# Handing out unnormalised x in the first block of a two-block fp32 transformer, with the inverse root multiplied in behind the products and half of the residual additions on GpSimd

## What is computed

```python
def rmsnorm(x, g):
    return x * rsqrt(mean(x * x, axis=-1) + EPS) * g

h = rmsnorm(x, norm_mix_pre[l])
a_in, b_x, b_b, b_c, q, k, v, gate_in = split(h @ w_in[l])
merged = ...                       # pooling, convolution and dilated attention, gated
x = x + rmsnorm(merged @ w_out[l], norm_mix_post[l])
h = rmsnorm(x, norm_mem_pre[l])
mem_n = rmsnorm(mem, norm_memkv[l])
x = x + rmsnorm(memory_cross_attention(h, mem_n, w_mq[l], w_mkv[l], w_mo[l]), norm_mem_post[l])
h = rmsnorm(x, norm_ffn_pre[l])
ua, ub = split(h @ w_up[l])
y = (silu(causal_dwconv(ua, conv_ffn_w[l])) * ub) @ w_down[l]
x = x + rmsnorm(y, norm_ffn_post[l])
```

## Time and profile before

| what | value |
|---|---|
| median of three runs | 3808.35 us (3804.64 to 3812.05) |
| the profiled execution | 3807.09 us, its span 3805.3 us |
| TensorE, products busy | 3605.1 us, 95% of the span |
| VectorE busy | 2018.6 us, 53% |
| ScalarE busy | 1504.8 us, 40% |
| GpSimd busy | 241.7 us, 6% |
| mean granted TensorE clock | 0.986 |

### The profile page before, as it was taken

The page is one execution under the profiler, slowest core; times in us unless marked ns, Lnnn a source line. Parts: engine busy times, 40 slices in busy tenths (PEclk is TensorE's granted clock), DMA queues, the critical chain, the costliest instruction groups (busy, mean ns, idle before and its releaser), DMA issues.

```text
span 3805.3 us, 52598 instructions
## 1 busy us (share of the span) xinstructions
PE 3605.1 (95%) x19348; PEld 2957.6 (78%) x19348; DVE 2018.6 (53%) x3396; ACT 1504.8 (40%) x2302; POOL 241.7 (6%) x384
## 2 busy tenths in 40 slices
PE   8999989999999998899999988899999998899998
PEld 6788876887787887688778776788888777667886
DVE  4634466777764455577774465442333444644344
ACT  4344354332324534533235366432122334743233
POOL 0000000001000000000000052000000002610000
PEclk9999999999999999999999999999999999999999
DMA  3222322446332233144551102111211122112322
GB/s 132 93 72 95 98 80 83 147 140 195 119 99 78 71 106 108 42 149 139 191 164 56 50 2 42 45 50 61 66 61 61 55 63 58 31 45 78 99 94 83
DMA packets 113071, 333.14 MB, mean 88 GB/s; under 512 B 32792, under 2 KB 33688, under 8 KB 112408
## 3 DMA queue, kind: packets, MB, share of 16 engines
q1 hardware_dynamic: 74112, 265.23, 21.6%
q0 software_dynamic: 14400, 52.44, 4.3%
q10 hardware_dynamic: 24408, 13.46, 1.6%
HBM read 328.99 MB, written 6.00 MB: 88 GB/s over the span
## 4 chain that ended last, share of the span: by engine, by line
PE 82%; DVE 8%; ACT 6%; issue 2%; DVEq 1%; POOL 0%; ACTq 0%; DMA 0%; POOLq 0%; SPq 0%
PE PS L602 14%; PE PS L604 13%; PE PS L603 13%; PE PS L984 10%; PE PS L985 10%; PE PS L987 10%; PE PS L1112 1%; PE PS L677 1%; PE PS L771 1%; ACT PB L1675 1%; ACT FULL_P L1675 1%; ACT L1366 1%; PE PS L783 1%; DVE HVAL L1958 1%; DVE Y L2371 1%
## 5 line engine op out<-in xcount | busy, mean ns | idle before, releaser
L1914 DVE TENSOR_TENSOR WL<-RAW,WH 128x1024 fp32r<-128x1024 f32 x494 | 604.5, 1224 | 573.5 <-ACT WH L1330 568.2
L1330 ACT ACTIVATE WH<-RAW 128x1024 fp32r<-128x1024 f32 x494 | 521.2, 1055 | 636.3 <-PE PS L987 350.2
L602 PE MATMUL PS<-HHI,WH 128*128 128x512 f32 x1632 | 651.2, 399 | 24.5 <-DVE HLO L1951 16.2
L604 PE MATMUL PS<-HHI,WL 128*128 128x512 f32 x1632 | 639.9, 392 | 0.0
L603 PE MATMUL PS<-HLO,WH 128*128 128x512 f32 x1632 | 638.0, 391 | 0.0
L984 PE MATMUL PS<-H2HI,WH 128*128 128x512 f32 (+1 forms) x1336 | 470.0, 352 | 0.0
L985 PE MATMUL PS<-H2LO,WH 128*128 128x512 f32 (+1 forms) x1336 | 446.6, 351 | 0.0
L602 PEld LDWEIGHTS PS<-HHI,WH 128*128 128x128 f32 x1632 | 307.4, 188 | 105.3 <-issue 19.7
L987 PE MATMUL PS<-H2HI,WL 128*128 128x512 f32 (+1 forms) x1336 | 387.4, 350 | 0.0
L604 PEld LDWEIGHTS PS<-HHI,WL 128*128 128x128 f32 x1632 | 307.1, 188 | 70.5
L603 PEld LDWEIGHTS PS<-HLO,WH 128*128 128x128 f32 x1632 | 307.3, 188 | 64.3 <-issue 0.5
(11 more groups left out here) (353 smaller groups left out, 5737.0 us busy)
## 6 DMA issues: line engine op xcount, KB each, us to landing
RAW<-in_stream SPq DMA_DIRECT2D x494, 512.0 KB, 3.6
MODW<-in_modw POOLq DMA_DIRECT2D x96, 512.0 KB, 4.6
bias_rows<-in_rpb ACTq DMA_DIRECT2D x8, 476.2 KB, 6.7
X<-in_x SPq DMA_DIRECT2D x4, 512.0 KB, 5.5
MEM<-in_mem ACTq DMA_DIRECT2D x2, 1024.0 KB, 4.9
CROW<-in_crow POOLq DMA_DIRECT2D x4, 512.0 KB, 4.7
BIAS<-bias_rows ACTq DMA_DIRECT2D x8, 224.0 KB, 5.0
GRID<-bias_rows ACTq DMA_DIRECT2D x8, 224.0 KB, 4.6
```

The lines of the kernel that those rows point to most:

```text
L602: nc.tensor.matmul(out, WH[:, slot, b * P:(b + 1) * P], hi, start=start, stop=False)
L604: return nc.tensor.matmul(out, WL[:, slot, b * P:(b + 1) * P], hi, start=False, stop=stop)
L1330: A(WH[:, d, :], RAW[:, s, :], ACT.Copy).then_inc(high_split, 1)
L1914: TT(WL[:, d, :], RAW[:, s, :], WH[:, d, :].bitcast(F32), ALU.subtract).then_inc(split_ready, 1)
```

## The change

It has these parts.

1. At M0, M1, F0 and F1 `raw_pair` takes the place of `sum_squares` and `chunk_pair`: for each chunk TensorE sums the squares (SQ_RAW, three buffers), then multiplies the unnormalised high and low parts with the first unit, and two chunks behind with the second. ScalarE makes x times gain in high precision, VectorE the rest (`raw_low`), as soon as each chunk of X is there.
2. At M0 and M1 only these two units are raw. They go to bank 1 and 4, and the normalised parts follow in HHI and HLO while they are read (`raw_read`). The next two units are a `chunk_pair` on them. The two U chunks are multiplied by the inverse root in the pooling. The weight splits for the next two units move into `norm_apply`; `memory_sums` stays behind the pair.
3. At Q0 and Q1 all four query units are raw. The pair comes ahead of the statistics product. VectorE multiplies each with the inverse root on its way out of PSUM.
4. At F0 and F1 all 44 units are raw. GpSimd multiplies UA and the result of Silu by the inverse root (RF): two operations of 128x512 for each pair of units. Its loads of modulation rows go between these. The second modulation reduction moves ahead of the last subtraction, and a weight split ahead of the convolution.
5. In the five residuals ahead of a raw norm, GpSimd adds every second chunk.
6. At the start, SyncE loads the parameters first and two weight units between the halves of x.

```diff
+SQ_RAW = place("SQ_RAW", [P, 3, T], at=S0)
+RF = place("RF", [P, T], at=S0 + 3 * T + 16)
@@ sync
+            sp.dma_start(PAR[:], params1).then_inc(par_in, 16)
             for j in range(4):
                 sp.dma_start(X[:, 2 * j:2 * j + 2, :], x[:, 2 * j:2 * j + 2, :]).then_inc(x_part[j], 16)
+                if j == 1:
+                    first_units(0, SPLIT_AHEAD)
+            first_units(SPLIT_AHEAD, RAW_SLOTS)
@@ gpsimd
+            def odd_additions(n):
+                for j in range(KB // 2):
+                    b = 2 * j + 1
+                    pool.wait_ge(y_scaled, n * (KB // 2) + j + 1)
+                    nc.gpsimd.tensor_tensor(X[:, b, :], X[:, b, :], Y[:, b, :], ALU.add).then_inc(x_odd, 1)
+                odd_additions(3 * l)
+                odd_additions(3 * l + 1)
+                load_modulation(0)
+                load_modulation(1)
+                for j in range(FF):
+                    pool.wait_ge(taken[0], UP_TAKEN[l] + j + 1)
+                    nc.gpsimd.tensor_tensor(UA[:, 0, 8:8 + T], UA[:, 0, 8:8 + T], RF[:], ALU.mult).then_inc(up_scaled, 1)
+                    if j:
+                        load_modulation(j + 1)
+                    pool.wait_ge(silu_ready, l * FF + j + 1)
+                    nc.gpsimd.tensor_tensor(FC[:, 0, :], FC[:, 0, :], RF[:], ALU.mult).then_inc(gate_scaled, 1)
+                for u in range(FF + 1, MOD_LAYER):
+                    load_modulation(u)
+                if l < DEPTH - 1:
+                    odd_additions(3 * l + 2)
@@ tensor
+            def raw_pair(hi, lo, sums, more, release=False, clock=18):
+                slots = [(m.n["units"] + x) % SLOTS for x in range(2)]
+                keep_clock(clock)
+                for slot in slots:
+                    set_in(slot)
+                for k in range(KB + RAW_LAG):
+                    if k < KB:
+                        if sums:
+                            m.add("sq")
+                            pe.wait_ge(sq_ready, m.at("sq"))
+                            nc.tensor.matmul(FLAT[:, 6 * T:7 * T], ONES[:], SQ_RAW[:, k % 3, :], start=k == 0, stop=k == KB - 1,
+                                             skip_group_check=True).then_inc(sq_summed, 1)
+                        if k == 0:
+                            pe.wait_ge(split_ready, m.at("units", 2))
+                        m.add("lo")
+                        pe.wait_ge(lo_ready, m.at("lo"))
+                        last = products(bank(3 * slots[0] + more), slots[0], k, hi[:, k, :], lo[:, k, :], k == 0, k == KB - 1)
+                        if k == KB - 1:
+                            unit_out(last)
+                    if k >= RAW_LAG:
+                        c = k - RAW_LAG
+                        last = products(bank(3 * slots[1] + more), slots[1], c, hi[:, c, :], lo[:, c, :], c == 0, c == KB - 1)
+                        if release and c < KB - 1:
+                            last.then_inc(raw_read, 1)
+                unit_out(last)
-                chunk_pair(HHI, HLO)
+                raw_pair(HHI, HLO, True, 1, release=True, clock=18 if l else 0)
+                chunk_pair(HHI, HLO, behind=1)
                 if l == 0:
                     memory_sums()
+                raw_pair(HHI, HLO, False, 1)
                 statistics(T)
-                chunk_pair(HHI, HLO)
                 for _ in range(HEADS - 2):
-                    chunk(HHI, HLO)
+                    chunk(HHI, HLO, behind=1)
-                sum_squares(T)
-                chunk_pair(HHI, HLO)
+                raw_pair(HHI, HLO, True, 0)
@@ scalar
+            def raw_and_squares(gain, arrived):
+                for k in range(KB):
+                    arrived(k)
+                    if k >= 3:
+                        act.wait_ge(sq_summed, m.at("sum", k - 2))
+                    A(SQ_RAW[:, k % 3, :], X[:, k, :], ACT.Square, scale=D ** -0.5).then_inc(sq_ready, 1)
+                    A(HHI[:, k, :], X[:, k, :], ACT.Identity, scale=gain(k)).then_inc(hi_ready, 1)
+            def x_landed(k):
+                if k == 4:
+                    for _ in range(SPLIT_AHEAD):
+                        split_high()
@@ scalar, at M0 and M1
+                root(T, summed=True)
+                unit_spent()
+                norm_high((0, 1))
+                unit_spent()
+                norm_high(range(2, KB))
+                for c in range(2):
+                    A(U[:, c, :], bank(3 * p + 1), ACT.Copy).then_inc(taken[p], 1)
                 if l == 0:
                     memory_squares()
@@ vector
+            def raw_low(k, gain):
+                m.add("hi")
+                dve.wait_ge(hi_ready, m.at("hi"))
+                STT(HLO[:, k, :], X[:, k, :], gain(k), HHI[:, k, :].bitcast(F32), ALU.mult, ALU.subtract).then_inc(lo_ready, 1)
             def norm_apply(gain):
                 for k in range(KB + 1):
+                    if k < KB - 1:
+                        m.add("rawr")
+                        dve.wait_ge(raw_read, m.at("rawr"))
+                    if k in (1, 3):
+                        split_low()
             def residual(gain, add, between=None, raw=None):
                 for k in range(0, KB, 2):
+                    scaled_y = [STT(Y[:, b, :], Y[:, b, :], par(gain + b), RS[:, 0:T], ALU.mult, ALU.mult) for b in (k, k + 1)]
+                        scaled_y[1].then_inc(y_scaled, 1)
+                        TT(X[:, k, :], X[:, k, :], Y[:, k, :], ALU.add).then_inc(x_ready, 2)
+                    if k and raw is not None:
+                        for b in (k - 2, k - 1):
+                            raw_low(b, raw)
+            for k in range(KB):
+                if k == 4:
+                    for _ in range(SPLIT_AHEAD):
+                        split_low()
+                raw_low(k, mix_gain(0))
@@ vector, in rope_tables
-                split_low()
                 dve.wait_ge(sin_ready, 2)
@@ vector, at the queries
+                def head_in(c):
+                    TT(QM[:, c, :], bank(3 * p + (c < 2)), RS[:, 0:T], ALU.mult).then_inc(taken[p], 1)
@@ vector, the up loop
+                        split_low()
+                        dve.wait_ge(up_scaled, m.at("ups"))
                         (the convolution as before)
+                        modulation(at(j), 0, b)
                         split_low()
+                        dve.wait_ge(gate_scaled, m.at("gts"))
                         TT(FT[:, 0, :], FC[:, 0, :], bank(3), ALU.mult).then_inc(taken[1], 1)
+                        modulation(at(j), 1, b)
+                        low(FLO[:, at(j), :], FT[:, 0:1, :], FHI[:, at(j), :])
```

More of the change, by code:

```diff
@@ L613, in unit_out, with set_in @@
                 m.add("units")
-            def set_in(p):
-                pe.wait_ge(taken[p], m.at(f"use{p}", 1))
+            def set_in(p, behind=0):
+                pe.wait_ge(taken[p], m.at(f"use{p}", 1 - behind))
                 m.add(f"use{p}")
@@ L1604, in _ @@
                         act.wait_ge(taken[1], m.at("use1", 1))
-                        A(FHI[:, bass.ds(2 * i + b, 1), :], FT[:, 0:1, :], ACT.Copy).then_inc(hi_ready, 1)
+                        A(FHI[:, b:b + 1, :] if first else FHI[:, bass.ds(2 * i + (b + 2), 1), :], FT[:, 0:1, :], ACT.Copy).then_inc(hi_ready, 1)
+                up_chunks(0, first=True)
+                with m.loop(act, FF // 2 - 1, units=4, use0=2, use1=2, conv=2, **QUAD) as i:
+                    up_chunks(i)
                 def of_down(k, dst, n):
@@ L2205, in _, with post @@
                     dve.drain()
[L2207 removed]
+                def post(gain, raw):
                     root_inverse(T)
[L2209 to L2213 removed]
+                    residual(gain, False, raw=raw)
                 for k in range(KB):
@@ L2297, in _ @@
                         m.add("use1")
-                        split_low()
-                        low(FLO[:, bass.ds(j, 1), :], FT[:, 0:1, :], FHI[:, bass.ds(j, 1), :])
-                        modulation(bass.ds(j, 1), 1, b)
+                        modulation(at(j), 1, b)
+                        low(FLO[:, at(j), :], FT[:, 0:1, :], FHI[:, at(j), :])
+                up_chunks(0, first=True)
+                with m.loop(dve, FF // 2 - 1, use0=2, use1=2, units=4, ups=2, gts=2, hi=2, modw0=1, modw1=1, **QUAD) as i:
+                    up_chunks(i)
                 m.add("units", DOWN_UNITS * KB)
```

182 lines of the change are left out of this document (107 added, 75 removed).

## The result

The changed kernel took 3827.0 us (median of 5 runs, 3824.66 to 3829.41), the kernel before on the same chip 3812.05 (5 runs, 3804.64 to 3813.81). The ratio is 1.0049 with a 95% interval of 1.0037 to 1.0062: slower, by 15 us in the medians and 18.7 by the ratio. The profiled execution took 3829.04 (span 3827.3, clock 0.978), 22.0 more than the one of before, so a ledger of the two traces must come to 22.0.

A forecast was written before the change was run, and what follows sets the result against it. TensorE, busy 95% of the span, was taken as the bound. Terms 2 x (-1.7 + 3.3) - 3.0 + 0 - 3.2 + 4.9 + 14.2 = +16.1 on 3807.7 gave 3824 us, 0.4% slower; range 3797 to 3838.

The forecast's parts named there:

- the largest term: M0, first block's start: sines behind the memory sums make unit 4's split late, done at 69.5; +14.2 us, bounds 8 and 17.
- the terms for Q0 and Q1: Query stages on unnormalised x: -3.0 us at Q1; 0 at Q0, bounds -3.0 and +5.3, with GpSimd's late first call there.
- that for the second block: Six head pairs of the second block lose the slowdown around GpSimd's 8.34 us wait: 24.0 instead of 27.2, -3.2 us.
- the second rival: M0: the sines do not gate unit 4, so M0 costs only 2; sum +3.9, 3812 us; chance 0.10.
- M1, +4.9 forecast: Second block's mixing start: normalisation moves behind the raw pair, unit 4's split behind the first pooling group; 47.9 against 43.0.
- The hold, taken as 1.26: Five residuals: each GpSimd addition holds VectorE up by 1.26 us, so a pair of chunks costs 4.8 instead of 2.7.
- The first rival: Five residuals: GpSimd does not hold VectorE up; 23 us less, sum -6.9, 3801 us; chance 0.24.
- front -1.7 forecast: F0 and F1 starts: third unit at 29.8, plus 1.8 for late fourth unit and clock, 31.6 against 33.3; -1.7 us each.
- loop's end +3.3: End of the up loop: last FLO done at 11.8, first down product at 12.3 instead of 8.98; +3.3 us each.
- 1.2 to spare: Up loop: VectorE finishes at 9.7, TensorE needs the bank at 10.96, so the loop costs nothing.
- From there TensorE runs on: pair 11.0: Query stage: after VectorE's work (31.7), TensorE does pair 11.0, fillers and statistics product 1.8, two units 11.0, ending at 55.5.
- In the second block the wait then goes: GpSimd's late first tensor_tensor meets Q0 instead, so its 8.34 us wait leaves the second block; -3.2 us.

The follow-up runs named there:

- Experiment 1: Changed kernel with ScalarE's memory root and sines and VectorE's rope tables later in the first block's start, same work: 3810.17 us, ratio 1.0003.
- experiment 2: Changed kernel with every odd addition of the residuals back on VectorE, none on GpSimd: 3821.7 us, ratio 1.0027.
- Experiment 3: Changed kernel with the second modulation reduction back behind the low part of the gated product in the up loop: 3855.82 us, ratio 1.0119.
- experiment 7: Kernel before plus an early GpSimd dummy: 3852.22 us; dummy of the late one's form, no tile moved: 3809.68; tiles shifted 32 bytes alone: 3854.48.

## Why the prediction was right, point by point

The forecast was 3824, slower, in a range of 3797 to 3838; measured were 3827.0 and a ratio of 1.0049. The direction, the size and the largest term were right. The rest is partly luck: the terms for Q0 and Q1 were wrong in opposite directions and cancelled, and that for the second block was wrong with nothing in the traces to make up for it. The traces differ by 22.0, so the forecast fits the medians better than it fits the two executions that it was worked out for.

- **M0, +14.2 forecast, +15.45 measured** in the trace. Unit 4's split ended at 70.7 (69.5 forecast), TensorE stood 13.38 (13). Experiment 1 shows the cause by taking it away: 17.5 us, of which 14.9 stand at unit 4 in its trace. Without this loss the kernel is level with the one before (1.0003), so it is what made the change a loss; the second rival (the sines don't gate) is what experiment 1 made true.
- **M1, +4.9 forecast, +4.25 measured.** Of it some 2.5 is GpSimd's hold (experiment 2).
- **The hold, taken as 1.26 with nothing below.** GpSimd's addition lasted 1.28 on average, VectorE's beside it 1.81 instead of 0.65: a hold of 1.16. The first rival falls. The Trainium skill (SBUF — State Buffer, Who interferes with whom) has the rule, that a VectorE instruction with two SBUF inputs and a reading GpSimd one exclude each other for a whole instruction, and by it VectorE's addition would have ended 0.65 behind GpSimd's; it ended 0.54 behind. The trace agrees to within 0.11. Experiment 3 shows both orders: GpSimd's product held to 2.17 where VectorE's reduction began first, the reduction held to 2.32 where it began second.
- **F0 and F1: front -1.7 forecast, -1.43 and -1.45; loop's end +3.3, +3.03 and +3.01.** Third unit 30.4 (29.8), wait for the last FLO 6.55 (6.8). For the late fourth unit and the clock together 1.8 was forecast; 30.37 for the third unit against an effective 31.86 (33.29 less 1.43) makes it 1.5. Experiment 1's run has the same code here, and its clock was back sooner in the pair and stayed up behind the wait: F0's third unit starts at 29.5, the stretch from there to the last UA copy takes 226.2 instead of 227.0, and the front gains 3.1 over the kernel before instead of 1.4. So the clock is about half of what the front could have gained.
- **Up loop, 0 forecast and measured.** "1.2 to spare" was right for this order and hid how little it takes to lose it (experiment 3).
- **Q1, -3.0 forecast, -0.54 measured.** The step that failed is "From there TensorE runs on: pair 11.0". VectorE's eighth split ended 32.1 after the start, as forecast (31.7), but TensorE was still with the keys and then with 18 fillers of 0.23, and began the pair at 33.2. From there to the end of the last unit it took 24.8 instead of 23.8: the second fillers and the statistics product, put at 1.8, took 2.8. The fillers ahead of the pair stand in the code, and the sum left them out because it thought TensorE idle there. The multiplication by the root on the way out, said to take as long as the copy, took 0.69 instead of 0.60.
- **Q0, 0 forecast with -3.0 to +5.3, measured -3.29**, just outside. GpSimd's late first call does not show at Q0. Its addition was ready to start at 498.29 and did; 8.34 from the end of its last load at 492.1 would have been 500.5.
- **Second block, -3.2 forecast, +0.8 between the traces.** The step that failed is "In the second block the wait then goes". It rested on the guess that the wait is the first `tensor_tensor` of the kernel; experiment 7 shows that neither an earlier call of it nor one of its exact form removes it.
- **Not in the sum:** +2.6 for products 2% slower up to 210 us, +0.8 from down stages at either clock, and -1.2 in three small steps ahead of F0, Q1 and F1. The first was there in experiment 2's run and not in experiment 3's, with the same code, and its cause is open. The second is the clock, which fell behind one of the two waits of 3.5 before and behind both of 6.55 after. The profiled execution of before was also 5 us under its median, so the traces differ by 22.0 where the medians differ by 15.

The net: the traces differ by 22.0 where the sum had 16.1. M0 cost 1.2 more and M1 0.7 less, Q0 and Q1 together gave 3.8 instead of 3.0, the second block lost 4.0 against its term, and what was not in the sum added 2.2. That the medians then differ by 15 and the ratio says 18.7 is the spread of single executions. One sum of chances is off by a little: from the rivals as listed, "same" comes to 0.22 and "slower" to 0.60, not 0.24 and 0.58.

## What to carry to other kernels

Where an engine's queue is written out by hand, a short side task (here two sines and a table of angles) belongs where its result is first needed; whatever lengthens the stage ahead of it makes every weight split behind it late. Moving it away brought the changed kernel 17.5 us and the kernel before 5.3. An idle GpSimd was no helper here to a busy VectorE, since both read the same memory at the same time: put the two side by side in one iteration and time the pair, not the one. And a change of several parts should be tried by parts: of this one only the query stages and, without GpSimd and by little, the feed-forward stages paid, and those parts with the later sines gave 0.9953.

## What the runs showed of the hardware

- Moving x and all tiles behind it by 32 bytes made TensorE's products of 128x512 in the first block come 0.2333 us apart instead of 0.2290, 2% slower, and the whole kernel 1.15% slower (ratio 1.0095 to 1.0134). In the kernel before, x began at a multiple of 64 bytes of a partition's memory. Which of the tiles matters was not tried. Anyone who adds a small tile should put it behind the others.
- VectorE and GpSimd held each other up in either order: VectorE's addition took 1.79 instead of 0.65 when both started together; GpSimd's product took 2.17 instead of 1.30 when VectorE's reduction had begun 0.2 before it, and the reduction 2.32 instead of 1.22 when it began 0.2 after.
- The granted clock behind the third unit's wait of 3 us was 0.68 in the changed kernel and 1.00 in experiment 1's run of the same code. Behind the down wait it fell in all 14 cases of about 6 us and more (0.50 to 0.71 in the first 5 us) and in seven of twelve of 3.5. It is worth 0.8 us at the third unit (227.0 against 226.2). In the kernels without shifted tiles the down stages took 129.5 to 132.6 in the 19 cases where it fell and 127.7 to 129.1 in the five where it stayed up, two of them with fillers. So two traces should not be compared without their windows.
